# Ten of sixteen gate products of a decoder layer as five pairs of seven block products, with the gates kept in DRAM

## The reference, cut to what matters

```python
h = rms_norm(x, norm1_g)
z = h @ w_in
cb, cc, ch, q, k, v, ga, gb = jnp.split(z, IN_OFFSETS, axis=-1)
u_ext = jnp.concatenate([conv_hist.astype(z.dtype), cc * ch], axis=1)
y_conv = (cb * short_conv(u_ext, conv_w)) @ w_conv_out
o, k_state, v_state = attn_fn(q..., k..., v...)
y_attn = o @ w_attn_out
mix = jax.nn.sigmoid(ga) * y_conv + jax.nn.sigmoid(gb) * y_attn
x = x + mix @ w_o
x = x + hier_moe(rms_norm(x, norm2_g), ...)
```

## Time and profile before

| what | value |
|---|---|
| median of 3 runs (lowest, highest) | 1683.44 us (1682.04, 1685.62) |
| span of the profiled execution, first to last instruction | 1682.9 us |
| that execution's own time | not recorded apart from its span; the span lies 0.5 us under the median of the runs |
| PE busy | 96% of the span |
| stage C | about 542 to 924 us |
| mean granted TensorE clock | 0.984 |

### The profile page before, as it was taken

The page is one execution under the profiler, slowest core; times in us unless marked ns, Lnnn a source line. Parts: engine busy times, 40 slices in busy tenths (PEclk is TensorE's granted clock), DMA queues, the critical chain, the costliest instruction groups (busy, mean ns, idle before and its releaser), DMA issues.

```text
span 1682.9 us, 26202 instructions
## 1 busy us (share of the span) xinstructions
PE 1613.2 (96%) x9427; PEld 1470.9 (87%) x9427; DVE 1104.4 (66%) x1967; ACT 845.3 (50%) x1234; POOL 231.8 (14%) x245
## 2 busy tenths in 40 slices
PE   5999999999999999999999999799999999999992
PEld 4999999999999999999999887688888888877781
DVE  5332588888887232114214676898998998888893
ACT  6011366666665321112112211678878778778783
POOL 1111011110110000000000111322122122232310
PEclk9999999999999999999999999799999999999996
DMA  5252111111112111131113712999999999999966
GB/s 151 72 137 79 55 51 51 50 49 39 50 50 88 30 39 50 50 137 52 50 50 126 291 71 82 357 393 379 370 377 376 380 375 379 369 373 370 361 222 224
DMA packets 131857, 305.30 MB, mean 181 GB/s; under 512 B 30404, under 2 KB 92080, under 8 KB 106936
## 3 DMA queue, kind: packets, MB, share of 16 engines
q1 hardware_dynamic: 115415, 267.76, 43.3%
q0 software_dynamic: 16384, 36.76, 7.5%
HBM read 282.81 MB, written 40.41 MB: 192 GB/s over the span
## 4 chain that ended last, share of the span: by engine, by line
PE 88%; DMA 6%; DVE 3%; issue 1%; ACT 1%; SPq 0%; DVEq 0%; POOLq 0%; ACTq 0%
PE bank L725 10%; PE bank L727 9%; PE bank L726 9%; PE bank L1071 8%; PE bank L1059 6%; PE bank L1061 6%; PE bank L1060 6%; PE bank L871 5%; PE bank L873 5%; PE bank L872 5%; DMA e_raw<-in_w_e_gate_dram 5%; PE bank L1019 2%; PE bank L1021 2%; PE bank L1023 2%; PE bank L832 2%; PE bank L1048 1%
## 5 line engine op out<-in xcount | busy, mean ns | idle before, releaser
L1967 DVE TENSOR_TENSOR e_lo<-e_raw,e_hi 128x2048 fp32r<-128x2048 f32 x192 | 433.4, 2288 | 55.4 <-ACT e_hi L1378 52.5
L1378 ACT ACTIVATE e_hi<-e_raw 128x2048 fp32r<-128x2048 f32 x192 | 364.5, 1920 | 50.0 <-DMA e_raw<-in_w_e_gate_dram 20.0
L1167 ACT ACTIVATE w_hi<-w_raw 128x1024 fp32r<-128x1024 f32 x68 | 71.6, 1054 | 325.5 <-DMA w_raw<-in_w_in_dram 182.2
L1493 DVE TENSOR_TENSOR w_lo<-w_raw,w_hi 128x1024 fp32r<-128x1024 f32 x68 | 83.2, 1223 | 203.4 <-ACT w_hi L1167 203.4
L1059 PE MATMUL bank<-e_hi,xT_hi 128*128 128x512 f32 x512 | 205.4, 401 | 3.4 <-DVE xT_lo L1978 3.4
L725 PE MATMUL bank<-h_hi,w_hi 128*128 128x344 f32 x624 | 202.5, 324 | 1.1 <-DVE h_lo L1512 1.1
L1061 PE MATMUL bank<-e_hi,xT_lo 128*128 128x512 f32 x512 | 201.5, 394 | 0.0
L1060 PE MATMUL bank<-e_lo,xT_hi 128*128 128x512 f32 x512 | 201.3, 393 | 0.0
L726 PE MATMUL bank<-h_lo,w_hi 128*128 128x344 f32 x624 | 199.6, 320 | 0.0
L727 PE MATMUL bank<-h_hi,w_lo 128*128 128x344 f32 x624 | 199.6, 320 | 0.0
L871 PE MATMUL bank<-h_hi,w_hi 128*128 128x344 f32 x576 | 190.2, 330 | 0.0
(11 more groups left out here) (351 smaller groups left out, 3164.3 us busy)
## 6 DMA issues: line engine op xcount, KB each, us to landing
e_raw<-in_w_e_gate_dram SPq DMA_DIRECT2D x64, 1024.0 KB, 19.9
e_raw<-in_w_e_up_dram SPq DMA_DIRECT2D x64, 1024.0 KB, 21.1
e_raw<-in_w_e_down_dram SPq DMA_DIRECT2D x64, 1024.0 KB, 21.6
w_raw<-in_w_in_dram SPq DMA_DIRECT2D x104, 256.0 KB, 3.3
a_spill<-y_sb POOLq DMA_DIRECT2D x8, 516.0 KB, 4.0
a_raw<-a_spill SPq DMA_DIRECT2D x2, 2064.0 KB, 12.9
x_tok<-in_x_prompt_dram SPq DMA_DIRECT2D x4, 1024.0 KB, 10.7
w_raw<-in_w_attn_out_dram SPq DMA_DIRECT2D x32, 128.0 KB, 3.0
```

Of the source, the lines that this page charges most:

```text
L1378: A.activation(e_hi[:, slot % 4, :], e_raw[slot][:, :], ACT.Copy).then_inc(e_hi_done, 1)
L1967: V.tensor_tensor(e_lo[slot][:, :], e_raw[slot][:, :], e_hi[:, slot % 4, :].bitcast(F32), ALU.subtract).then_inc(e_lo_done, 1)
```

## The change

Sixteen gate units stay, but only the first 6 (PLAIN) are made as before. The other 10 are made in 5 pairs. A pair takes two units as the rows, the two halves of the 1024 inputs as the inner blocks, and two halves of 516 tokens (HALF) as the columns of a 2 x 2 block product, and makes it with seven block products in place of eight. A block product has 4 k-tiles x 3 matmuls x 2 quarters of 258 tokens (QTR). Four of the seven use sums of blocks of h (`t_raw`, made by DVE once, split into `t_hi` by ACT and `t_lo` by DVE), and four use sums of blocks of the weights (`sums_of_blocks`, for each pair). The seven products leave PSUM as one copy by ACT and additions by DVE (`add_product`, 14 instructions a pair) into the buffers `gate` and `st2`; ACT takes the sigmoid there. Products go round the 8 banks, so product m + 4 waits until product m has left.

All gates are written to DRAM (`g_dram`) and read back later: gb in one go into `mix`, ga two and then one at a time. The 16 output projections now all come after the gates: units u = 0 to 7 on the attention output, whose split parts `c_hi`, `c_lo` lie where `h_hi`, `h_lo` were, and 8 to 15 on the conv output. `mix0_hi`, `mix0_lo` move within the ring, and the second of the first expert chunks is loaded last in place of the fourth. All loops of stage C are written out.

The diff, cut to its core:

```diff
+PLAIN, PAIRS = 6, 5
+HALF, QTR = T // 2, T // 4
...
+    g_dram = nc.dram_tensor("gate_spill", (P, 2 * KT, T), F32).ap()
...
+        t_raw = at("t_raw", R5, [4, 4, HALF])
+        t_lo = at("t_lo", R5, [4, 4, HALF], F32R)
+        w_pair = at("w_pair", RING + 20480, [KT, 2, P])
+        p_raw = [at(f"p_raw{i}", RING + 20480 + 4096 * i, [KT, P]) for i in range(2)]
...
+            def spill_plain(n):
+                for c in range(3):
+                    sp.wait_ge(gate_out, 3 * n + c + 1)
+                    sp.dma_start(g_dram[:, n, CH * c:CH * c + CH], gate[:, CH * c:CH * c + CH]).then_inc(gate_spilled[c], 16)
...
+                if p > 0:
+                    sp.wait_ge(b_lo_done, B_LO_FROM + 7 * p - 1)
...
+            for n in range(PLAIN):
                 cols(1 - n % 2, w_in_t, n + COL_GB // P, c_freed(n))
-            for n in range(AHEAD, 2 * AHEAD):
-                out_cols(1 - n % 2, n - AHEAD, c_freed(n))
-            with sp.Fori(AHEAD, KT) as j:
-                cols(1, w_in_t, j + COL_GB // P, c_freed(j * 2))
-                out_cols(0, j, c_freed(j * 2 + 1))
-
-            for n in range(2):
-                cols(1 - n, w_in_t, COL_GA // P + n, c_freed(16 + n))
-            sp.wait_ge(chunk_done, 111 + 48)
-            for x in range(2):
-                sp.dma_start(a_raw[:, 4 * x:4 * x + 4, :], a_dram[:, 4 * x:4 * x + 4, :]).then_inc(a_loaded[x], 16)
...
+                if n == PLAIN - 1:
+                    load_pair(0)
+                if n:
+                    spill_plain(n - 1)
+            spill_plain(PLAIN - 1)
+            load_pair(1)
+            for p in range(PAIRS):
+                spill_part(p, 0, 0, 1)
+                spill_part(p, 1, 1, 2)
+                spill_part(p, 1, 0, 3)
+                if p + 2 < PAIRS:
+                    load_pair(p + 2)
+                if p == PAIRS - 2:
+                    sp.wait_ge(b_lo_done, B_LO_FROM + 7 * PAIRS - 1)
+                    load_part(0, None)
+                    load_part(1, None)
+                if p == PAIRS - 1:
+                    sp.wait_ge(product_done, PRODUCT_FROM + 14 * PAIRS - 2)
...
+                    sp.dma_start(mix[:, 0:1, :], g_dram[:, 0:1, :]).then_inc(mix_loaded[0], 16)
+                    sp.dma_start(mix[:, 1:KT, :], g_dram[:, 1:KT, :]).then_inc(mix_loaded[1], 16)
+                spill_part(p, 0, 1, 4)
+            for u in range(2, 2 * KT):
+                load_part(u, 129 + 3 * (u - 1))
+                if u == 2:
+                    sp.wait_ge(o_lo_done, 5)
...
+                        sp.dma_start(gates2[par][:, :], g_dram[:, KT + par, :]).then_inc(ga_loaded[par], 16)
+                if u > KT + 1:
+                    sp.wait_ge(chunk_out, 135 + 3 * (u - KT - 1))
+                    sp.dma_start(gates2[u % 2][:, :], g_dram[:, u, :]).then_inc(ga_loaded[u % 2], 16)
...
-            for n in range(AHEAD):
-                unit_c(n, 1 - n % 2, h_hi, h_lo, n if n else None, 0, caches)
-            for n in range(AHEAD, 2 * AHEAD):
-                unit_c(n, 1 - n % 2, o_hi, o_lo, AHEAD if n == AHEAD else None, n - AHEAD, ready=o_lo_done if n == AHEAD else None)
-            with pe.Fori(AHEAD, KT) as j:
-                unit_c(j * 2, 1, h_hi, h_lo, None, j)
-                unit_c(j * 2 + 1, 0, o_hi, o_lo, j + 1, None)
-
-            unit_c(2 * KT, 1, h_hi, h_lo, None, KT)
...
+            def product(p, m, x):
+                out = bank[2 * ((7 * p + m) % 4) + x][:, 0:QTR]
+                for k in range(4):
+                    xh, xl = moving(m, k, x)
+                    pe.matmul(out, b_hi[m][:, k, :], xh, start=k == 0, stop=False)
+                    pe.matmul(out, b_hi[m][:, k, :], xl, start=False, stop=False)
+                    mm = pe.matmul(out, b_lo[m][:, k, :], xh, start=False, stop=k == 3)
+                mm.then_inc(product_done, 1)
...
+            pe.wait_ge(so_stored, 1)
+            for p in range(PAIRS):
+                for m in range(7):
+                    pe.wait_ge(b_lo_done, B_LO_FROM + 7 * p + m + 1)
+                    if p == 0 and m in (1, 3, 4, 5):
+                        pe.wait_ge(t_lo_done, T_LO_FROM + {1: 1, 3: 3, 4: 3, 5: 4}[m])
+                    for x in range(2):
+                        q, old = (7 * p + m - 4) // 7, (7 * p + m - 4) % 7
...
+                        elif old == 0:
+                            pe.wait_ge(part_copied, COPIED_FROM + 2 * q + x + 1)
+                        else:
+                            pe.wait_ge(part_added, ADDED_FROM + left(q, old, x))
+                        product(p, m, x)
...
+                        pe.wait_ge(o_lo_done, (2, 3, 5)[c])
...
+            def high_of_t(i):
+                act.wait_ge(t_raw_done, T_RAW_FROM + max(i + 1, 2))
+                A.activation(t_hi[:, i, :, :], t_raw[:, i, :, :], ACT.Copy).then_inc(t_hi_done, 1)
...
+            def high_block(p, m):
+                if p > 0:
+                    act.wait_ge(product_done, PRODUCT_FROM + 14 * (p - 1) + 2 * m + 2)
+                if m in (0, 2, 5):
+                    act.wait_ge(pair_loaded, PAIR_FROM + 32 * p + 32)
+                else:
+                    act.wait_ge(s_done, S_FROM + 4 * p + {1: 2, 3: 3, 4: 1, 6: 4}[m])
...
+                act.wait_ge(part_added, ADDED_FROM + left(p, 2, 1))
+                gated(gate, 0)
+                if not last:
+                    high_block(p + 1, 2)
+                    high_block(p + 1, 3)
+                    high_block(p + 1, 4)
...
+            act.wait_ge(product_done, PRODUCT_FROM + 14 * PAIRS)
+            high_of_o(slice(0, 8), slice(HALF, 2 * CH))
+            high_of_o(slice(0, 4), slice(2 * CH, T))
+            high_of_o(slice(4, 8), slice(2 * CH, T))
+            for u in range(1, 2 * KT - 1):
+                high_part(u + 1)
...
+            def combine(i, first, second, rest):
+
+                for j, (a, b, op) in enumerate([(first, second, ALU.subtract)] + rest):
+                    for g in range(2):
+                        ks = slice(2 * g, 2 * g + 2)
+                        dst = t_raw[:, i, ks, :]
+                        ins = V.tensor_tensor(dst, dst if a is None else a[:, ks, :], b[:, ks, :], op)
+                        if j < len(rest):
+                            step.after(ins)
+                ins.then_inc(t_raw_done, 1)
+
+            def t_one():
+                combine(0, high[:, lo_half, later], high[:, lo_half, before],
+                        [(None, low[:, lo_half, later], ALU.add), (None, low[:, lo_half, before], ALU.subtract)])
...
             ins.then_inc(q_new_done, 1)
+            t_one()
             split_lo(U_C + 2, 1)
+            t_two()
             dve.wait_ge(kcT_psum, 4)
             step.after(V.memset(q_of[:, :, :, :], 0.0))
             for b in range(B8):
...
+            split_lo(U_C + 4, 1)
+            dve.wait_ge(states_out, 16 * 7)
+            t_three()
+            t_four()
+            low_of_t(1, 1)
+            low_of_t(0, 2)
+            split_lo(U_C + 5, 0)
+            low_of_t(2, 3)
+            low_of_t(3, 4)
...
+            def sums_of_blocks(p):
+
+                dve.wait_ge(pair_loaded, PAIR_FROM + 32 * p + 32)
+                a11, a12, a21, a22 = w_pair[:, 0:4, 0, :], w_pair[:, 4:8, 0, :], w_pair[:, 0:4, 1, :], w_pair[:, 4:8, 1, :]
+                V.tensor_tensor(s_raw[0][:, :, :], a21, a22, ALU.add).then_inc(s_done, 1)
+                dve.wait_ge(s_done, S_FROM + 4 * p + 1)
+                V.tensor_tensor(s_raw[1][:, :, :], s_raw[0][:, :, :], a11, ALU.subtract).then_inc(s_done, 1)
+                V.tensor_tensor(s_raw[2][:, :, :], a11, a21, ALU.subtract).then_inc(s_done, 1)
+                dve.wait_ge(s_done, S_FROM + 4 * p + 2)
+                V.tensor_tensor(s_raw[3][:, :, :], a12, s_raw[1][:, :, :], ALU.subtract).then_inc(s_done, 1)
...
+            sums_of_blocks(0)
+            dve.wait_ge(chunk_done, 111 + 3 * PLAIN)
+            for m in range(7):
+                low_block(0, m)
...
+            for p in range(PAIRS):
+                last, n0 = p == PAIRS - 1, 14 * p
+                if not last:
+                    sums_of_blocks(p + 1)
+                dve.wait_ge(part_copied, COPIED_FROM + 2 * p + 2)
...
+                add_product(p, 1, gate, gate, 1, 0)
+                if not last:
+                    low_block(p + 1, 0)
+                    low_block(p + 1, 1)
+                else:
+                    low_of_o(1, slice(0, 4), slice(0, HALF))
+                add_product(p, 2, gate, gate, 0, 0)
...
+            low_of_o(3, slice(0, 8), slice(HALF, 2 * CH))
+            low_of_o(4, slice(0, 4), slice(2 * CH, T))
+            low_of_o(5, slice(4, 8), slice(2 * CH, T))
...
+            for u in range(KT):
+                if u > 0:
+                    low_part(u + 1)
+                projected(PLAIN + u, u)
...
```

(64 more changed lines are left out.)

314 lines of the change are left out of this document (209 added, 105 removed).

## The result

The changed kernel took **1692.62 us** (median of 4 runs, 1690.92 to 1695.54) against 1684.53 for the kernel before in the same comparison: ratio 1.0049, 95% interval 1.0034 to 1.0063. It is slower by about 8 us, where 1685 and "in effect no change" were forecast; the time lies in the range of 1675 to 1694. The profiled execution is the fastest of the four (1690.92 us, span 1689.3), 6.4 us longer than the span before. L814 to L816 are the unit matmuls of L725 to L727, L1022 is L933, L1033 is L944.

The account below looks back on a forecast made before the run. PE, busy 96% of the span, was taken to bound the kernel; savings of -12.9 and -0.9 against waits, transitions and clock summed to +1.7 us on the 1682.9 span, hence 1685 us, in effect no change, range 1675 to 1694.

Parts of the forecast that it names:

- the clock term: At L933: the granted clock falls in the idle stretch before it, so L933 runs partly at half speed, +1.2 us.
- Rival 3: The clock falls in both A and B, +1.2 and +2.4 us more, 1688.6 us; chance 0.15.
- A: Before L933: PE waits for q_of, which stands behind t_one and t_two on DVE, +4.9 us.
- B: Before unit 5: its split stands on DVE behind t_three, t_four and two low parts, +3.6 us.
- Waits by DVE's written order: In stage C: DVE works in written order, so added instructions delay what PE wants next; A +4.9, A2 +1.2, B +3.6.
- the late load: Before L933: unit 2's weights come 1.3 us later, as SP first waits for a sigmoid and issues a spill.
- A2: At L944: pn8T stands behind the split of unit 3's weights, which a spill makes late, +1.2 us.
- Pairs: Gates of stage C: each pair takes 168 matmuls of 0.1194 us, 20.06 in place of 22.64; -12.9 us for five.
- rival 4: In the pairs: the seven products run at the pace of 344 columns, +32 us in all; chance 0.05.
- Rival 2: At sums_of_blocks: the weight load bounds the pair loop and PE waits, +8, 1693 us; chance 0.17.
- Transitions: Into the pairs, a wait for the first low part, +0.9 us; out of them, for c_hi and c_lo, +0.8.
- Wait C: Fourth attention projection, u = 3: its weights queue behind a_raw and two ga gates, +2.9 us.

Follow-up runs that it names:

- e8: Kernel before, with the memset of q_of done 13 times in place of once, so that L933 waits: 1698.45 us, ratio 1.0076.
- e9: Kernel before, with the memset of q_of done 9 times in place of once, so that L933 waits less long: 1694.35 us, ratio 1.0058.
- e7: Changed kernel with 18 filler matmuls on a spare bank in front of the wait for q_of: 1686.51 us, ratio 1.0004.
- e1: Changed kernel with t_two moved behind the instructions that make q_of on DVE: 1683.37 us, ratio 0.9986.
- e3: Changed kernel with DVE's split of unit 5's weights moved ahead of the two low parts of t: 1688.83 us, ratio 1.0022.
- e4: Changed kernel with the spills of the six plain gate units issued by GpSimd in place of SyncE: 1688.43 us, ratio 1.0016.
- e5: Changed kernel with the first two ga gates read back one projection later: 1691.09 us, ratio 1.0030.
- e10: Changed kernel with a_raw issued ahead of the weights of u = 2 in place of behind them: 1701.89 us, ratio 1.0099.
- e2: Changed kernel with 36 filler matmuls put into the wait for q_of, filling 8.1 us: 1693.95 us, ratio 1.0049.

## Why the prediction was right in part and wrong in sum

**The step that failed is the clock term.** The prediction took +1.2 with bounds 0 to 5.9 ("L933 runs at half speed for some of its 5.95 us"); the trace has +7.9. The kernel before with nothing but a late `q_of` has 6.5 and 6.4 (e8, e9), and filling the wait won 7.6 net (e7). Two readings were missing. First, the clock fell within the wait (0.92 from 568 to 570), so that all of L1022 ran at half speed, not a part. Second, the 64 small matmuls did not bring it back in 11 us, though the busy column shows PE full; it came back only behind dense ones, and the first 19 of those were slow too. The bound of 5.9 counted the damage only up to the end of L933, and was no bound. The trace of the kernel before already had the pattern: the clock falls in a small block, as the earlier trace rows show, and is back only behind it, when the first ten dense matmuls (from 589.40 on) have run slow.

```profile
590.00:592.00 2.00, 2.00 (x9) 2.00 (x8) 0.00 (x0) 0.00 (x0) 0.00 (x0) 0.50 0.00 0
592.00:594.00 2.00, 2.00 (x14) 2.00 (x13) 0.00 (x0) 0.00 (x0) 0.00 (x0) 0.92 0.03 8
```

This should have set the upper end.

**Rival 3** had the mechanism but the same price, 1688.6 for A and B together. For B its 2.4 us were near: 1.5 by the traces in which the clock fell there. The Trainium skill, "TensorE: Matmul & The Clock Gate", Part 1, says that the low clock is the default and only sustained activity releases it. The runs agree in that the clock did not come back before dense matmuls ran; but L1022 kept PE full for 11.22 us and did not release it, which the sentence alone would not have told. The full charge by that rule was 2.4 us in the prediction, as it was worked out over 5 us only.

**Waits by DVE's written order** were right in place and near in size. A: 4.3 against 4.9, as `t_one` took 7.4 us and not 7.8, `t_two` 4.9 and not 5.1, and the late load 1.1 and not 1.3. B: 2.6 against 3.6, of which shorter durations of the same kind are 0.6. A2 is 0.4 in the profile of the changed kernel and 0.9 in e1 and e3, against a predicted 1.2. Of the 1.3 us from the spills in SP's queue, e4 shows 1.1.

**Pairs**: -12.3 against -12.9, at 0.1201 us a matmul and not 0.1194. At the pace of 344 columns it would be 0.157, so rival 4 fell. Rival 2, the load bound, did not come: `w_pair` landed 4.9 us after its issue at the median, under the 5.5 assumed, and PE waits nowhere in the pairs. Transitions: 1.6 against 1.7.

**Wait C** was oversized (1.2 against 2.9) and one of its causes wrong: the two ga gates, 2.6 us of the working, show no effect (e5). That loads stand in line in issue order was right (e10).

**Direction.** The chances put 0.40 on "same" and 0.38 on "slower", and the forecast's own range of 1681 to 1689 was missed by 3.6 us. The errors of the sum are +6.7 (clock), -4.1 (A, A2, B, C), +0.5 (pairs and transitions), +1.0 (start and end of the stage) and +0.6 (behind it): 1.7 + 4.7 = 6.4, the difference of the spans. That the time lies within 1675 to 1694 is luck: the waits were priced 4.1 too high, and without that error the clock would have taken it to about 1696.7. The ratio stands for 8; the profiled execution is 1.7 under the median of its four. A fall of the clock at wait B, which it was spared, would cost 1.5 and could be this difference; that was seen in traces of other kernels, not in one of this kernel.

## What to carry to other kernels

A saving on TensorE is worth its row only while nothing makes TensorE idle: here 12 us of saved matmuls were lost to one wait of 4 us on an in-order DVE, since the clock that fell with it cost nearly twice the wait (7.9 us, and 6.4 to 6.5 in six other traces, behind waits of 3.1 to 6.2). Price such a wait as its length plus all that runs at half clock until dense matmuls have brought the clock back, small matmuls between included; and before adding work to an engine that is 27% busy, look at which instruction behind it TensorE wants next. If a wait can't be moved away, filler matmuls of the same length can win back most of the clock's part (7.6 us here); filled to twice its length (e2) they won nothing.
